# The value projection as seven products of quarters, in place of whole token tiles, in a two-layer hybrid encoder on one core

## What is computed

```python
h = rms_norm(x, norm_mix_g)
u = h @ w_in                      # split among four mixers
# A neighbourhood attention (needs q, k and v), B bidirectional mLSTM (q, k, v, o and gates),
# C convolution module, D grouped-query attention
x += (sum over b of sigmoid(h @ w_gate_b) * (mixer_b @ w_branch_b)) @ w_out
x += hierarchical_moe(rms_norm(x, norm_ffn_g))
```

## Time and profile before

| | |
|---|---|
| time, median of 3 runs | 2131.52 us (2131.32 to 2131.7) |
| span of the profiled execution | 2130.5 us (no time of its own is listed; the median of the runs is 1.0 us above this span) |
| PE busy | 2009.6 us, 94% |
| DVE busy | 1030.5 us, 48% |
| ACT busy | 527.0 us, 25% |
| POOL busy | 348.7 us, 16% |
| instructions | 24257 |

### The profile page before, as it was taken

One profiled execution on the slowest core, in us unless ns is written; L12 is line 12 of the kernel. 1 busy time (PEld: TensorE's weight loads), 2 busy tenths in 40 slices (PEclk: granted clock), 3 DMA queues, 4 the chain that ended last, 5 costly groups with the idle time before them and its releaser, 6 DMA issues. The chain is left out here.

```text
span 2130.5 us, 24257 instructions
## 1 busy us (share of the span) xinstructions
PE 2009.6 (94%) x8820; PEld 1264.9 (59%) x8820; DVE 1030.5 (48%) x1898; ACT 527.0 (25%) x1126; POOL 348.7 (16%) x278
## 2 busy tenths in 40 slices
PE   7999999999999997999699999999999999979991
PEld 4555565555665555888455556645556555568871
DVE  3588415353445975111266882344434379541114
ACT  3233213345320010111123341134453100111111
POOL 2322220111210011000233222102221100210003
PEclk9999999999999998999899999999999999989996
DMA  5555647111226415998641111121121271189965
GB/s 214 196 205 229 240 180 302 55 70 69 80 80 273 158 40 218 400 369 318 225 171 48 76 70 74 61 79 70 70 79 60 99 299 68 60 328 391 374 230 188
DMA packets 67397, 362.97 MB, mean 170 GB/s; under 512 B 5808, under 2 KB 6192, under 8 KB 54064
## 3 DMA queue, kind: packets, MB, share of 16 engines
q1 hardware_dynamic: 42656, 278.57, 34.3%
q10 hardware_dynamic: 17712, 57.68, 6.8%
q0 software_dynamic: 6912, 25.17, 3.1%
HBM read 250.24 MB, written 112.20 MB: 170 GB/s over the span
## 5 line engine op out<-in xcount | busy, mean ns | idle before, releaser
L732 PE MATMUL bank<-hT,ring 128*128 128x384 f32 x1056 | 360.7, 491 | 2.9 <-ACT gbuf L923 2.9
L732 PE MATMUL bank<-x,ring 128*128 128x384 f32 x1056 | 361.7, 491 | 1.0 <-POOL ring L1240 1.0
L732 PEld LDWEIGHTS bank<-hT,ring 128*128 128x128 f32 x1056 | 195.6, 190 | 149.3 <-issue 26.9
L732 PEld LDWEIGHTS bank<-x,ring 128*128 128x128 f32 x1056 | 194.9, 190 | 147.5 <-issue 26.1
L896 ACT ACTIVATE sums<-bank 128x384 f32<-128x384 f32 x132 | 64.8, 491 | 292.9 <-PE bank L732 291.2
L1054 DVE SCALAR_TENSOR_TENSOR reg_a<-cvx,pp,reg_a 128x783 f32<-128x783 f32 x120 | 128.9, 1074 | 4.3
L710 PE MATMUL bank<-ring,hT 128*128 128x272 f32 (+1 forms) x384 | 127.9, 493 | 0.0
L1032 DVE SCALAR_TENSOR_TENSOR gbuf<-bank,sums 128x384 f32<-128x384 f32 x96 | 53.5, 558 | 134.9 <-PE bank L732 101.4
L1848 DVE SCALAR_TENSOR_TENSOR prob<-prob,bank 128x256 f32<-128x256 f32 x30 | 12.6, 421 | 215.1 <-ACT prob L1622 215.1
L710 PEld LDWEIGHTS bank<-ring,hT 128*128 128x128 f32 x384 | 72.5, 190 | 51.6 <-issue 43.7
L1594 ACT ACTIVATE prob<-x 128x1024 f32<-128x1024 f32 x12 | 12.7, 1059 | 332.7 <-DVE x L1725 332.7
(11 more groups left out here) (282 smaller groups left out, 3118.9 us busy)
## 6 DMA issues: line engine op xcount, KB each, us to landing
ring<-in_wd SPq DMA_DIRECT2D x26, 2048.0 KB, 8.3
blocks<-hT SPq DMA_DIRECT2D x16, 3072.0 KB, 21.4
gate_dram<-gbuf ACTq DMA_DIRECT2D x64, 384.0 KB, 2.3
ring<-gate_dram SPq DMA_DIRECT2D x16, 1536.0 KB, 6.9
oT<-in_we SPq DMA_DIRECT2D x8, 2048.0 KB, 12.7
wide<-in_we SPq DMA_DIRECT2D x8, 2048.0 KB, 12.2
reg_b<-in_we SPq DMA_DIRECT2D x8, 2048.0 KB, 12.0
ring<-in_we SPq DMA_DIRECT2D x8, 2048.0 KB, 12.3
```

Of the source, the lines that this page charges most:

```text
L732: mm = nc.tensor.matmul(bank[i % 2][:, 0:HALF], w[:, k, :], a[:, k, :], start=(k == 0 and r in (0, 1, 3)), stop=(k == 3), skip_group_check ...
```

## The change

The value projection is done as seven products as well, two token tiles together: tile p and tile p + 3, for p = 0, 1, 2. The features are split in two halves (4 blocks each) and the 512 columns in two halves of 256. Here the activations are the stationary operand (128 tokens) and the weights or their sums the moving one (256 columns). GpSimd forms four weight sums in a new step `prep nv`, placed behind `cnorm`: the first in `ring` itself, the others in buffers that are free then (`cvx`, `probT`, `oT`). The eviction is now shared: ScalarE copies products 0, 2 and 3 to `sums` and product 6 to `nav`; VectorE adds a bank and `sums` for products 1 (to `nav`), 4 and 5 (to `mlv`). The columns of ones are written by ScalarE in one go ahead of its first copy. `mofold` and the first scores stand behind step 12, which is product 5 of the second pair. `gates` and `bias` stay ahead of all of it.

```diff
@@ schedule
     add("cnorm")
+    add("prep", "nv", 0)
...
     add("gates")
     add("bias")
-    for u in range(PROJ_UNITS["nv"]):
-        add("proj", "nv", u)
-        if u == 0:
+    for i in range(T // 2 * PRODUCTS):
+        add("proj", "nv", i // PRODUCTS, i % PRODUCTS)
+        if i == 0:
             add("turn", "cv", 4)
             add("turn", "cv", 5)
-        if u == 3:
+        if i == 12:
             add("mofold")
             first_scores("na")
@@ mix_tensor
+            def values(i, name, p, r):
+                wait_chunk(pe, layer, chunk_of(name, p))
+                pe.wait_ge(proj_ev[i % 2], i // 2)
+                if r >= 2:
+                    pe.wait_ge(nv_sums, {2: 2, 3: 2, 4: 3, 5: 3, 6: 4}[r])
+                w, a = ((nv_b11, quarter[0][0]), (nv_b21, quarter[0][1]), (nv_t2, s_of[1]), (nv_b12, s_of[0]),
+                        (nv_t3, s_of[2]), (nv_b22, s_of[3]), (nv_t4, quarter[1][1]))[r]
+                for k in range(4):
+                    mm = nc.tensor.matmul(bank[i % 2][:, 0:BW], a[:, k, p * P:(p + 1) * P], w[:, k, :],
+                                          start=(k == 0 and r in (0, 1, 3)), stop=(k == 3), skip_group_check=True)
+                mm.then_inc(proj_mm, 1)
@@ mix_scalar
-                    done(activate(nav[:, u, :], b[:, 0:BW], ACT.Copy))
-
-                    done(activate(mlv[:, u, :, HD], ones[:, 0:HEADS], ACT.Copy))
-                    ins = activate(mlv[:, u, :, 0:HD], b[:, BW:2 * BW].rearrange("p (h c) -> p h c", h=HEADS), ACT.Copy)
...
+                b = bank[i % 2][:, 0:BW]
+                if (p, r) == (0, 0):
+                    act.wait_ge(pv_mm, at_over)
+                    for t in range(T):
+                        done(activate(mlv[:, t, :, HD], ones[:, 0:HEADS], ACT.Copy))
+                if r in (0, 2, 3, 6):
+                    act.wait_ge(proj_mm, i + 1)
+                    to = nav[:, p + T // 2, :] if r == 6 else sums[:, 1 if r == 2 else 0, 0:BW]
+                    out(activate(to, b, ACT.Copy), i)
@@ mix_vector
+                if r in (1, 4, 5):
+                    if (p, r) == (0, 1):
+                        dve.wait_ge(turn_mm, at[("turn", "cv", T - 1)] + 1)
+                    dve.wait_ge(proj_mm, i + 1)
+                    held = i - 3 if r == 5 else i - 1
+                    dve.wait_ge(proj_ev[held % 2], held // 2 + 1)
...
+                    stt(to, view(bank[i % 2][:, 0:BW]), 1.0, view(sums[:, 1 if r == 5 else 0, 0:BW]), ALU.mult, ALU.add
+                        ).then_inc(proj_ev[i % 2], 1)
@@ mix_gpsimd
+                wait_chunk(pool, layer, CHUNK_NAMES.index("nv"))
+                pool.wait_ge(conv_done, 1)
+                done(tensor_(nv_b12, nv_b12, nv_b11, ALU.subtract), nv_sums)
+                done(tensor_(nv_t2, nv_b22, nv_b12, ALU.subtract), nv_sums)
+                pool.wait_ge(pv_mm, at[("attend", "at", T - 1, HEADS // 2 - 1)] + 1)
+                done(tensor_(nv_t3, nv_t2, nv_b11, ALU.subtract), nv_sums)
+                pool.wait_ge(cn_done, 1)
+                done(tensor_(nv_t4, nv_b21, nv_t2, ALU.subtract), nv_sums)
```

More of the change, by code:

```diff
@@ L92, in tile_group @@
     return 0 if tile < GROUPS[0][1] else 1
-PROJ_UNITS = {"at": 6, "nv": 6, "mo": 6, "mg": 2}
+PROJ_UNITS = {"at": 6, "mo": 6, "mg": 2}
 PAIRED = ("cv", "gate", "ml", "na")
@@ L347, in t2_of @@
             return (cvx[:, 0, 0:512] if name == "gate" and g >= 6 else dg[:, 1, :]).rearrange("p (k n) -> p k n", k=4)
+        nv_w = ring[:, CHUNK_NAMES.index("nv") % 2, :].rearrange("p (k n) -> p k n", k=KD)
+        nv_b11, nv_b12, nv_b21, nv_b22 = nv_w[:, 0:4, 0:BW], nv_w[:, 0:4, BW:], nv_w[:, 4:8, 0:BW], nv_w[:, 4:8, BW:]
+        nv_t2, nv_t3, nv_t4 = (
+            a.rearrange("p (k n) -> p k n", k=4)
+            for a in (cvx[:, :, :].rearrange("p j t -> p (j t)")[:, 512:512 + 4 * BW],
+                      probT[:, :, :].rearrange("p s c -> p (s c)"), oT[:, 0:2, :].rearrange("p a b -> p (a b)")[:, 0:4 * BW]))
         def out_of(name, g, n, hf):
@@ L412, in program @@
                                                       sem("x_back"))
-        cols_zero = sem("cols_zero")
+        cols_zero, nv_sums = sem("cols_zero"), sem("nv_sums")
         ctanh_done, lsig_ln, decay_done = sem("ctanh_done"), sem("lsig_ln"), sem("decay_done")
@@ L765, in attend @@
                 if name == "na" and tile == 0:
-                    evicted(pe, at[("proj", "nv", T - 1)])
+                    evicted(pe, at[("proj", "nv", T // 2 - 1, PRODUCTS - 1)])
                 if i >= 1:
@@ L854, in mix_tensor @@
                     product(i, *key)
+                elif kind == "proj" and key[0] == "nv":
+                    values(i, *key)
                 elif kind == "proj" and key[0] == "mg":
@@ L872, in proj @@
                 act.wait_ge(proj_mm, i + 1)
-                if name == "nv" and u == 0:
-                    act.wait_ge(turn_mm, at[("turn", "cv", T - 1)] + 1)
-                    act.wait_ge(pv_mm, at_over)
                 if name == "mg":
                     ins = activate(top_rows[:, half], b[:, 0:HALF], ACT.Identity, bias=pp[:, PP_GB:PP_GB + 1])
-                elif name == "mo":
+                else:
                     if u == 0:
@@ L883, in proj, with values @@
                                    b[:, BW:BW + GATE_ROWS].rearrange("p (q r) -> p q r", q=4), ACT.Copy)
-                else:
-                    done(activate(nav[:, u, :], b[:, 0:BW], ACT.Copy))
-                    done(activate(mlv[:, u, :, HD], ones[:, 0:HEADS], ACT.Copy))
-                    ins = activate(mlv[:, u, :, 0:HD], b[:, BW:2 * BW].rearrange("p (h c) -> p h c", h=HEADS), ACT.Copy)
                 out(ins, i)
+            def values(i, name, p, r):
+                b = bank[i % 2][:, 0:BW]
[7 more added lines that the diff above has]
+                    out(activate(to, b, ACT.Copy), i)
             def product(i, name, g, r):
@@ L1032, in product, with values @@
                     stt(out_of(name, g, n, hf), b, scale, sums[:, 1 if r == 5 else 0, :], ALU.mult, ALU.add
+                        ).then_inc(proj_ev[i % 2], 1)
+                    dve.wait_ge(proj_ev[i % 2], i // 2 + 1)
+            def values(i, name, p, r):
+                if r in (1, 4, 5):
[4 more added lines that the diff above has]
+                    dve.wait_ge(proj_ev[held % 2], held // 2 + 1)
+                    heads = lambda a: a.rearrange("p (h c) -> p h c", h=HEADS)
+                    to = nav[:, p, :] if r == 1 else mlv[:, p if r == 5 else p + T // 2, :, 0:HD]
+                    view = (lambda a: a) if r == 1 else heads
+                    stt(to, view(bank[i % 2][:, 0:BW]), 1.0, view(sums[:, 1 if r == 5 else 0, 0:BW]), ALU.mult, ALU.add
                         ).then_inc(proj_ev[i % 2], 1)
@@ L1206, in mix_vector @@
                         product(i, *key)
+                    elif key[0] == "nv":
+                        values(i, *key)
                 elif kind == "rope":
@@ L1234, in prep, with prep_values @@
                 done(tensor_(t2_of(name, g), b22, b12, ALU.subtract), t_done)
+            def prep_values():
+                wait_chunk(pool, layer, CHUNK_NAMES.index("nv"))
[6 more added lines that the diff above has]
+                done(tensor_(nv_t4, nv_b21, nv_t2, ALU.subtract), nv_sums)
             def product(i, name, g, r):
@@ L1252, in mix_gpsimd @@
                     power(4 + i, 8 * i, 2 * GROUPS[key[0]][1])
+                elif kind == "prep" and key[0] == "nv":
+                    prep_values()
                 elif kind == "prep":
```

## The result

The changed kernel takes 2172.48 us (median of 5 runs, 2169.67 to 2173.56) beside 2131.7 of before: ratio 1.0183, 95% interval 1.0171 to 1.0195. It is 40.8 us slower; 2168.8 had been forecast. The profiled execution has a span of 2170.7 us and a time of 2172.53.

What follows compares the result with a forecast made beforehand. The value stage was taken as bound by TensorE. A layer: -4.9 matmuls, +3.0 and +15.7 waits, +2.2 scores, +2.7 clock, 18.6 us; two layers add 37.3 to the 2130.5 span, plus 1.0: 2168.8 us, range 2157 to 2180.

Steps and rivals of the forecast that it cites:

- Matmuls, -4.9 us: Value stage on TensorE: 168 rows of 256 columns, 36.3 us, replace 96 of 512, 41.2 us; 4.9 us less a layer.
- the interpolation from 272 and 512 columns: TensorE's value rows: 0.229 us at 272 columns and 0.429 at 512 give about 0.216 us for 256 columns.
- The estimate of 0.32 us for 256 columns: Opposing price for TensorE's value rows from the skill's bfloat16 figures: stage 54 us, a loss of 13 us a layer.
- Waits, 3.0 + 15.7 = 18.7 us: TensorE idles 3.0 us before the third value product for ScalarE, 15.7 before the fourth for VectorE behind `gates` and `bias`.
- `mofold` and scores, 2.2 us: `mofold`, first scores, table load and exponentials delay an eviction after product (1,5); TensorE waits 2.2 us before product (2,1).
- Clock, 2.7 us: After the 15.7 us idle TensorE's granted clock falls to 0.50; costs 2.7 us a layer, taken between 1.7 and 3.0.
- GpSimd, 0 us: GpSimd's four weight sums, 2.5 to 2.9 us each, finish before the value stage needs them; price 0, VectorE contention put at 0.

Runs made afterwards that it cites:

- e5: Changed kernel with `bias` behind `cnorm` and `gates` cut in five pieces, four of them between the value products; 2143.24 us, ratio 1.0055 to the kernel before.
- e7: As e6, but `bias` among the `na` products instead of behind `cnorm`; 2126.15 us, ratio 0.9971 to the kernel before.
- e8: Changed kernel with `bias` among the `na` products, `gates` whole behind all value products, dependent transposes six pairs later; 2163.26 us, ratio 1.0147 to the kernel before.
- e2: Changed kernel with `mofold` moved behind all value products; 2169.15 us, ratio 1.0168 to the kernel before.
- e3: Changed kernel with unused filler matmuls on TensorE, 3 before the third product and 17 before the fourth; 2166.48 us, ratio 1.0168 to the kernel before.
- e1: Changed kernel with `bias` moved from behind `gates` to behind `cnorm`; 2168.07 us, ratio 1.0171 to the kernel before.
- e4: Kernel before with GpSimd's four unused sums added behind `cnorm`, the first value unit waiting for them; 2132.5 us, ratio 0.9998 to the kernel before.
- e6: As e5, with the copies of ones behind product 4 of pair 2 and `mofold` behind all value products; 2132.51 us, ratio 0.9995 to the kernel before.

## Why the prediction was right

Step by step, layer 0:

- **Matmuls, -4.9 us.** A product at full clock is 1.73 us in every kernel, 0.216 us a row, so the interpolation from 272 and 512 columns held, and the weight loads are hidden. The estimate of 0.32 us for 256 columns from the two figures of the Trainium skill (TensorE: Matmul & The Clock Gate, Back-to-back issue gap) is wrong for these float32 rows.
- **Waits, 3.0 + 15.7 = 18.7 us.** Two holes of 2.92 and 13.99 us were found, and the third product took 3.5 instead of 1.73 between them: from the end of (0,1) at 343.6 to 364.22 is 20.6 us with 1.73 of work in it, 18.9 lost. The chain was as forecast. The 15.7 itself was not seen: the clock had fallen already in the first hole, which the prediction did not reckon with, and the slow third product filled 1.7 us of the second hole. That this cost nothing was luck of the order. That e5 takes 15 us out of the stage and e7 all of it, with the same products, shows that the order on VectorE is the cause; e8 shows that the uncut block makes TensorE wait in another place as well.
- **`mofold` and scores, 2.2 us.** 2.10; e2 takes 1.63 of it away.
- **Clock, 2.7 us.** 3.1 (1.82 and 1.28 on two products), shown by e3 to be the clock; 0.4 more than the term, and 0.1 above its upper bound of 3.0. That it came so near is partly luck: behind the long wait the same two products lost 1.6 us in layer 1 of e2 and 2.5 and 2.6 in e1.
- **GpSimd, 0 us.** Right for the changed kernel and for e4. The sums take 2.36 us alone and some 3.75 beside VectorE's rows, where 2.5 to 2.9 had been forecast; the last ends at 338.74 in layer 0 and, in layer 1, at 1406.45, 1.5 us ahead of the stage. The contention itself is larger than I had read from one row. In layer 1 of the changed kernel two `cnorm` rows of 1.76 us took 3.79, and two of GpSimd's sums beside them 3.74 and 3.77:

```profile
1390.69 1.76 DVE L1139 TENSOR_TENSOR reg_a<-reg_a,small 128x1536 f32<-128x1536 f32 x1 [1.58 <-POOL small L1268]
1392.49 3.79 DVE L1140 TENSOR_TENSOR reg_a<-reg_a,rows 128x1536 f32<-128x1536 f32 x1
1396.31 3.79 DVE L1141 TENSOR_TENSOR reg_a<-reg_a,rows 128x1536 f32<-128x1536 f32 x1
```

```profile
1392.00 2.66 POOL L1286 TENSOR_TENSOR ring<-ring 128x1024 f32<-128x1024 f32 x1 [1.41 <-DMA ring<-in_wd]
1394.74 3.74 POOL L1287 TENSOR_TENSOR cvx<-ring 128x1024 f32<-128x1024 f32 x1
1398.56 3.77 POOL L1289 TENSOR_TENSOR probT<-cvx,ring 128x1024 f32<-128x1024 f32 x1
```

These rows too fit turns and not a shared pace: each one waits for the end of the other engine's and then needs its own 1.76 or 2.36 us. So VectorE's row of 1392.49 waits for the sum that ends at 1394.66 and would end 1.76 later, at 1396.42 (1396.28 in the trace), and the sum of 1394.74 waits for that and would end at 1398.64 (1398.48).

The Trainium skill (GPSIMD Engine Reference, Key points) says that GpSimd shares SBUF interfaces with VectorE, and that VectorE instructions with two SBUF inputs, or in a 2-port perf mode, contend. The rows with two inputs agree, with more than double the time. The slack of `cnorm` swallowed it; e1 and e5, which use up that slack for `bias`, are where it reached TensorE.

By these terms a layer is 18.9 + 2.1 + 3.1 - 4.9 = 19.2 and some 0.2 of seams, where 18.6 had been forecast. Of the 3.7 us by which the time exceeds the forecast, 1.6 are these in two layers, 1.3 lie outside the stages, less than the differences between the profiled executions there, and 0.8 come from the step from span to time: the prediction added 1.0 us, and the profiled execution shows 1.8 (2170.7 and 2172.53).

## What to carry to other kernels

Before an eviction is given to another engine, look at what that engine's queue holds at this point in the program: an engine that is 48% busy can still be closed for 20 us in a row, and a matmul saving of 4.9 us a layer stood against 24.1 us of waits and slow clock. Long uncut work on a queue that now evicts banks should be cut into pieces that fit between two evictions, as in e5 to e7; putting the block elsewhere whole only moved the wait (e8). And an idle slot on VectorE was only free where GpSimd was idle as well: `bias` delayed `gates` in e1, e5 and e6, and not in e7.

## What the runs showed that I had not expected

- Beside GpSimd's sums VectorE slows not only on instructions with two SBUF inputs: the `gates` row L1157, a minimum with one input, took 2.60 us for 0.56 (e1). Whether it runs in a 2-port mode no row here shows.
- The same hole of 2.1 us had no effect on the granted clock in the changed kernel (1.00 behind it) and halved it in layer 0 of e3 (0.51) and e5 (0.50), at a price of 1.7 us. Holes of 2.8 to 3.2 us before the third product halved it in each case shown here.
- In the profile the wait that mattered most had no name ("issue", 33.9 us in four waits). The row of the evicting engine that starts late is what names it.
